# One gather per layer into slots sorted by expert, range copies for each pair, and expert outputs accumulated in four PSUM banks

## The reference, cut to what matters

```python
for l in range(DEPTH):                      # 2 layers
    h = h + mixer_l(rms_norm(h, ln_mix[l]))
    xn = rms_norm(h, ln_ffn[l])
    h = h + hier_moe(xn, ...)
# hier_moe: top-1 of 4 groups, top-2 of its 8 experts, 32 experts in all
g_sel = argmax(xt @ w_rg + b_rg)
top_w, top_i = top_k(softmax(e_logits of g_sel), 2)
for e in range(32):
    hh = silu(xt @ w_gate[e]) * (xt @ w_up[e])      # 1024 -> 512
    y = y + combine[:, e:e+1] * (hh @ w_down[e])    # 512 -> 1024
```

## Time and profile before

| | us |
|---|---|
| median of 3 runs (1334.38 to 1337.42) | 1336.81 |
| the profiled execution's own time | 1337.13 |
| its span, first to last instruction | 1335.3 |
| gather of layer 0 starts, last scatter of layer 0 ends | 169.08, 673.93 |
| gather of layer 1 starts, last scatter of layer 1 ends | 832.56, 1328.28 |
| TensorE busy | 1275.1 (95%) |
| VectorE, ScalarE, GpSimd busy | 287.7, 189.7, 162.6 |
| moved by DMA | 444.44 MB |

### The profile page before, as it was taken

The page is one execution under the profiler, slowest core; times in us unless marked ns, Lnnn a source line. Parts: engine busy times, 40 slices in busy tenths (PEclk is TensorE's granted clock), DMA queues, the critical chain, the costliest instruction groups (busy, mean ns, idle before and its releaser), DMA issues.

```text
span 1335.3 us, 15013 instructions
## 1 busy us (share of the span) xinstructions
PE 1275.1 (95%) x5526; PEld 630.2 (47%) x5526; DVE 287.7 (22%) x621; ACT 189.7 (14%) x445; POOL 162.6 (12%) x392
## 2 busy tenths in 40 slices
PE   6999899999999999999989998999999999999997
PEld 4776464343434344334367764643434343443432
DVE  1664411111111111111122335011111111111112
ACT  1244111010101011201012231110101010110101
POOL 3002011101010102010010000111010101121000
PEclk9999989999999999999999999999999999999999
DMA  6944578899999999799793335659999999999980
GB/s 226 386 180 166 213 321 319 355 413 414 409 423 406 422 409 423 308 415 401 305 358 126 127 142 214 278 234 403 408 423 411 422 403 423 414 423 409 408 342 32
DMA packets 65684, 444.44 MB, mean 333 GB/s; under 512 B 7188, under 2 KB 10384, under 8 KB 13024
## 3 DMA queue, kind: packets, MB, share of 16 engines
q1 hardware_dynamic: 63728, 438.09, 81.1%
q0 software_dynamic: 1040, 2.61, 0.7%
q10 hardware_dynamic: 864, 3.02, 0.6%
HBM read 442.59 MB, written 1.09 MB: 332 GB/s over the span
## 4 chain that ended last, share of the span: by engine, by line
PE 94%; DVE 3%; ACT 1%; issue 1%; DMA 1%; POOL 0%; DVEq 0%; POOLq 0%; SPq 0%; ACTq 0%
PE PS L1342 34%; PE PS L1351 17%; PE PS L1362 9%; PE PS L1094 9%; PE PS L1321 8%; PE PS L1210 4%; PE PS L1098 3%; PE PS L1308 2%; PE PS L1378 1%; PE PS L1106 1%; PE PS L1165 1%; PE PS L1073 1%; DVE mix L1020 1%; PE PS L1194 1%; ACT gain_att L712 1%
## 5 line engine op out<-in xcount | busy, mean ns | idle before, releaser
L1342 PE MATMUL PS<-ring,xT 128*64 128x512 f32 x1392 | 312.8, 595 | 0.0
L1342 PEld LDWEIGHTS PS<-ring,xT 128*64 128x64 f32 x1392 | 96.1, 137 | 206.9 <-issue 206.9
L1351 PE MATMUL PS<-ring,gain_att 128*64 128x512 f32 x768 | 171.4, 595 | 7.5 <-ACT gain_att L712 7.5
L1362 PE MATMUL PS<-mix 128*128 128x512 f32 x256 | 126.8, 618 | 1.7 <-ACT mix L721 1.7
L1094 PE MATMUL PS<-xT,ring 128*128 128x256 f32 (+1 forms) x512 | 120.8, 389 | 0.7 <-issue 0.7
L1034 DVE TENSOR_TENSOR h<-PS,h 128x512 f32<-128x512 f32 x128 | 88.5, 692 | 143.0 <-PE PS L1362 142.8
L1321 PE MATMUL PS<-mix,xn 128*128 128x256 f32 x448 | 116.2, 412 | 0.0
L1321 PEld LDWEIGHTS PS<-mix,xn 128*128 128x128 f32 x448 | 109.4, 335 | 11.4 <-issue 11.4
L1094 PEld LDWEIGHTS PS<-xT,ring 128*128 128x128 f32 (+1 forms) x512 | 96.1, 192 | 22.1 <-issue 7.2
L1351 PEld LDWEIGHTS PS<-ring,gain_att 128*64 128x64 f32 x768 | 53.0, 137 | 108.8 <-issue 97.3
L460 POOL TENSOR_TENSOR sm<-sm 128x1 f32<-128x1 f32 x46 | 8.9, 193 | 743.8 <-PE PS L1384 730.5
(11 more groups left out here) (194 smaller groups left out, 886.7 us busy)
## 6 DMA issues: line engine op xcount, KB each, us to landing
ring<-in_moe_w_up SPq DMA_DIRECT2D x96, 1024.0 KB, 9.6
ring<-in_moe_w_down SPq DMA_DIRECT2D x96, 1024.0 KB, 10.3
ring<-in_moe_w_gate SPq DMA_DIRECT2D x94, 1024.0 KB, 8.6
wo<-in_moe_w_gate SPq DMA_DIRECT2D x34, 1024.0 KB, 9.6
wo<-in_moe_w_down SPq DMA_DIRECT2D x30, 1024.0 KB, 12.0
wo<-in_moe_w_up SPq DMA_DIRECT2D x24, 1024.0 KB, 8.2
ring<-in_c_w_in SPq DMA_DIRECT2D x12, 1024.0 KB, 8.5
ring<-in_ab_w_in SPq DMA_DIRECT2D x9, 1024.0 KB, 10.1
```

Source lines behind the costliest of these rows:

```text
L1342: last = mm(PS[e * SLOTS:(e + 1) * SLOTS, 2 + part, :], (xg if n < 2 else xg2)[:, k, x_cols], w[e][:, kk, :], start=(k == 0), stop=(k == N ...
L1351: last = mm(PS[e * SLOTS:(e + 1) * SLOTS, 6 + b, :], hidT[:, k, e * SLOTS:(e + 1) * SLOTS], w[e][:, 512 * b:512 * b + 512], start=(k == 0) ...
L1362: mm(PS[:, b], pickT[:, t], ye[:, 512 * b:512 * b + 512], start=True, stop=True).then_inc(s_sca[l], 1)
```

## The change

Names: PICKED = 512 is the number of picks of a layer. `acts` is one tile that holds `xn`, `xT` and `kon` behind one another. `xg_all` lies over `xn` and `xT` and has 8 blocks of 512 slots.

- VectorE counts the picks of each expert, sums them up to the start of each expert's range, and from this gets for each token the two slots of its two picks (`pos`, `late`, `early`). It writes `pick_all`, 512 columns for each of the two token tiles.
- TensorE gathers all picks of the layer once, 8 blocks with 2 matmuls of 512 columns each. ScalarE and VectorE copy the blocks in turn to `xg_all`.
- For each pair ScalarE copies, for each of the two experts, 64 columns of all 8 blocks from the start of its range to `xg` (`window`). The start is read into a register of ScalarE. Columns behind the range belong to the next experts; `pickw` has zeros there.
- The wide fills, `pick2`, `xg2` and the gathers of pair 1 are gone; GpSimd makes only `pickw`.
- The scatters accumulate in banks 0, 1, 4 and 5 over all pairs of the layer. Those of pair i run in pair i + 1, two ahead of the turns of `hid` and two behind. The four adds to `h` come once, at the end of the layer. The turns now go to banks 2 and 3.
- No up chunk of the next pair is drawn forward. `xT` is no single-use place any more, so four are left.
- The turned bias of layer 1 comes one pair later (LAST 3 instead of 4).
- Rows of the weights are laid out so that block k of `xn` is 128 neighbouring columns instead of every eighth column. This is done on the host for the large weights; the router weights `wr` are now read in pieces of 16 and 128 bytes instead of 128 bytes and 1 KB.

The core of the diff, a line of "..." where something is left out:

```diff
-LAST = 4
-AHEAD = 2
+LAST = 3
+PICKED = SEQ * TOP_EXPERTS
...
+GATHER_BANK = (0, 1, 2, 3, 6, 7, 0, 1)
+BLOCK = (4, 5, 6, 7, 0, 2, 1, 3)
+Y_BANK = (0, 1, 4, 5)
...
+        xg_all = acts[:, 0:NK * PICKED].rearrange("p (b n) -> p b n", b=NK)
...
-                sp.wait_ge(s_lg[l], 2)
-                chunk(l, 1, 1, OUT_CHUNKS + ONCE - 2)
...
-                pool.dma_start(wr[:, :, 0:GROUPS], w_rg[l].rearrange("(p k) g -> p k g", k=NK)).then_inc(s_wr[l], 16)
-                pool.dma_start(wr[:, :, GROUPS:ROUTES], w_re[l].rearrange("(p k) g -> p k g", k=NK)).then_inc(s_wr[l], 16)
+                pool.dma_start(wr[:, :, 0:GROUPS], w_rg[l].rearrange("(k p) g -> p k g", k=NK)).then_inc(s_wr[l], 16)
+                pool.dma_start(wr[:, :, GROUPS:ROUTES], w_re[l].rearrange("(k p) g -> p k g", k=NK)).then_inc(s_wr[l], 16)
...
+                def window(base, e, blocks=slice(0, NK)):
+                    src = acts[:, bass.ds(base, NK * PICKED)].rearrange("p (b n) -> p b n", b=NK)
+                    act.activation(xg[:, blocks, e * SLOTS:(e + 1) * SLOTS], src[:, blocks, 0:SLOTS], ACT.Copy).then_inc(s_xg[l], 1)
+                def experts(i, first=False, final=False):
+                    if not final:
+                        base = [base_of(i + 1, e) for e in range(AT_ONCE)]
                     act.wait_ge(s_used[l], i * CHUNKS + UP_CHUNKS)
                     if not first:
                         act.wait_ge(s_ht[l], i)
                     act.activation(hid, PS[:, 2], ACT.Silu).then_inc(s_si[l], 1)
-                    if first:
-                        gathered_copy(1, 0)
-                    if odd and not final:
-                        wide_copy(i + 1, 0)
-                        wide_copy(i + 1, 1)
+                    if not final:
+                        act.wait_ge(s_used[l], i * CHUNKS + 2 * UP_CHUNKS)
+                        for e in range(AT_ONCE):
+                            window(base[e], e)
                     act.wait_ge(s_ht[l], i + 1)
-                    act.activation(hidT, PS[:, 4].rearrange("p (k n) -> p k n", k=NF), ACT.Copy).then_inc(s_hT[l], 1)
-                    if first:
-                        gathered_copy(1, 1)
-                    if odd and not final:
-                        wide_copy(i + 1, 2)
-                        wide_copy(i + 1, 3)
+                    act.activation(hidT, PS[:, 2].rearrange("p (k n) -> p k n", k=NF), ACT.Copy).then_inc(s_hT[l], 1)
                     act.wait_ge(s_used[l], i * CHUNKS + CHUNKS)
...
+                link(dve.tensor_copy(counts, PS[:, 5, 0:EXPERTS]))
+                link(dve.tensor_tensor_scan(starts, counts, counts, 0.0, ALU.add, ALU.max))
+                link(dve.tensor_tensor(starts, starts, counts, ALU.subtract))
+                link(dve.tensor_tensor(pos, chose, starts.unsqueeze(1).broadcast_to((P, NT, EXPERTS)), ALU.mult))
+                link(dve.tensor_tensor(pos, pos, rank, ALU.add))
+                link(dve.tensor_reduce(late, pos, AX.X, ALU.max))
+                link(dve.tensor_reduce(both, pos, AX.X, ALU.add))
+                link(dve.tensor_tensor(early, both, late, ALU.subtract))
+                link(dve.tensor_scalar(early2, early, -float(SEQ), None, ALU.add))
+                iota = kon[:, 4 * P:4 * P + SEQ]
                 for t in range(NT):
...
+                    a, b = pick_all[:, t, 0:SEQ], pick_all[:, t, SEQ:2 * SEQ]
+                    dve.tensor_scalar(a, iota, late[:, t:t + 1], None, ALU.is_equal)
+                    link(dve.tensor_scalar(b, iota, float(SEQ), late[:, t:t + 1], ALU.add, ALU.is_equal))
+                    dve.scalar_tensor_tensor(a, iota, early[:, t:t + 1], a, ALU.is_equal, ALU.add).then_inc(s_pk, 1)
+                    dve.scalar_tensor_tensor(b, iota, early2[:, t:t + 1], b, ALU.is_equal, ALU.add).then_inc(s_pk, 1)
+                for j in range(MAX_PASSES):
+                    ins = dve.tensor_scalar(bases_f[0:1, j * EXPERTS:(j + 1) * EXPERTS], starts[0:1], float(SLOTS * j), float(PICKED),
+                                            ALU.add, ALU.min)
+                link(ins)
+                dve.tensor_copy(bases, bases_f[0:1]).then_inc(s_base, 1)
+                weights(l, 1, s_wt)
...
+                def gather(k):
+                    if k >= 6:
+                        pe.wait_ge((s_xa, s_xd)[k % 2], 4 * l + 1)
+                    for t in range(NT):
+                        if k == 0:
+                            pe.wait_ge(s_pk, 4 * l + 2 * t + 2)
+                        last = mm(PS[:, GATHER_BANK[k]], xn[:, t, k * P:(k + 1) * P], pick_all[:, t], start=(t == 0), stop=(t == NT - 1))
+                    last.then_inc(s_g, 1)
...
+                def scatter(q, first=False, final=False):
                     t, b = q // 2, q % 2
...
+                    last = mm(PS[:, Y_BANK[q]], pickT[:, t], ye[:, 512 * b:512 * b + 512], start=first, stop=final)
+                    if final:
+                        last.then_inc(s_sca[l], 1)
+                def ye_there(i):
+                    pe.wait_ge(s_ya[l], i + 1)
+                    pe.wait_ge(s_yd[l], i + 1)
+                    pe.wait_ge(s_pkT[l], i + 1)
+                def pair(i, n, rounds=0, first=False, second=False):
+                    for c in range(2 * UP_CHUNKS):
                         up_chunk(i, first, n, rounds, c)
...
+                    if not first:
+                        ye_there(i - 1)
+                        scatter(0, second)
+                        scatter(1, second)
                     pe.wait_ge(s_hi[l], i + 1)
+                    for k in range(NF):
+                        last = nc.tensor.transpose(PS[:, 2, k * P:(k + 1) * P], hid[:, k * P:(k + 1) * P], ident)
+                    last.then_inc(s_ht[l], 1)
                     if not first:
...
+                        scatter(2, second)
+                        scatter(3, second)
                     pe.wait_ge(s_pw[l], i * PICKS + PICKS)
...
                     for t in range(NT):
...
+                        last = nc.tensor.transpose(PS[:, 3, t * P:(t + 1) * P], pickw[:, t], ident)
                     last.then_inc(s_pkt[l], 1)
...
                     pe.wait_ge(s_hT[l], i + 1)
...
                     for k in range(NF):
                         down_chunk(n, rounds, k)
...
+                for k in range(NK):
+                    gather(k)
                 pair(0, 0, first=True)
...
+                pair(1, 1, second=True)
```

More of the change, by code:

```diff
@@ L70 @@
 PICKS = NT * AT_ONCE
-WIDE = 2 * AT_ONCE
-FILLS = 4
 UNITS = 16
@@ L258, in build @@
         now, now_w, now_slots = at(4936, NT, AT_ONCE), at(4940, NT, AT_ONCE), at(4944, SLOTS)
-        xg2 = xT
-        pick2 = at(1536, NT, WIDE * SLOTS)
-        now2, now2_w = at(5008, NT, WIDE), at(5016, NT, WIDE)
+        pos, counts, starts = at(3584, NT, EXPERTS), at(3648, EXPERTS), at(3680, EXPERTS)
+        bases_f, bases = at(3712, MAX_PASSES * EXPERTS), drop0[0:1, :].bitcast(INT32)
+        late, both, early, early2 = (at(5008 + 2 * j, NT) for j in range(4))
         isc, cand, over, same = (bias[:, 12 + j] for j in range(4))
@@ L500, in pick_rows @@
                     pool.tensor_copy(now_slots, kon[:, bass.ds(i // PAIRS * SLOTS + 4 * P, SLOTS)]).then_inc(s_now[l], 1)
[L501 to L508 removed]
+                    pool.wait_ge(s_now[l], i * 3 + 3)
+                    if not first:
+                        pool.wait_ge(s_pkt[l], i)
                     carry_waits(1)
@@ L1015, in _, with experts @@
                 ranks(l)
-                def experts(i, first):
+                for k in range(1, NK, 2):
+                    gathered_copy(l, k)
+                def experts(i):
                     dve.wait_ge(s_used[l], i * CHUNKS + 2 * UP_CHUNKS)
@@ L1353, in down_chunk @@
                     last.then_inc(s_used[l], 1)
-                def scatter(i, q):
+                def scatter(q, first=False, final=False):
                     t, b = q // 2, q % 2
-                    if q < 2:
-                        pe.wait_ge((s_ya, s_yd)[b][l], i + 1)
-                    else:
-                        pe.wait_ge(s_add[l], i * 4 + (q - 1))
-                    mm(PS[:, b], pickT[:, t], ye[:, 512 * b:512 * b + 512], start=True, stop=True).then_inc(s_sca[l], 1)
-                def pair(i, n, rounds=0, first=False, final=False):
-                    for c in range(0 if first else AHEAD, 2 * UP_CHUNKS):
-                        up_chunk(i, first, n, rounds, c)
-                    if first:
-                        gather(1, 0)
-                    if n % 2 == 1 and not final:
-                        wide_fill(i + 1, 0)
-                        wide_fill(i + 1, 1)
+                    last = mm(PS[:, Y_BANK[q]], pickT[:, t], ye[:, 512 * b:512 * b + 512], start=first, stop=final)
+                    if final:
+                        last.then_inc(s_sca[l], 1)
@@ L1380, in pair @@
                     pe.wait_ge(s_pw[l], i * PICKS + PICKS)
-                    if not first:
```

(20 more changed lines are left out.)

237 lines of the change are left out of this document (86 added, 151 removed).

## The result

| | before | after |
|---|---|---|
| median, us | 1335.6 (1334.19 to 1337.42, 4 runs) | 1271.35 (1270.6 to 1273.3, 4 runs) |
| the profiled execution's time and span | 1337.13, 1335.3 | 1270.6, 1268.4 |
| TensorE busy | 1275.1 (95%) | 1166.0 (92%) |

The ratio is **0.952, 95% interval 0.9502 to 0.9539**: faster, as forecast, and inside the range of 1246 to 1285. The predicted 1259 is 12 us too low. In spans it is 1257.2 against 1268.4, 11.2 us.

What follows compares the result with a forecast made beforehand. It took TensorE and the loads as full together, the loads binding after the change: span 1335.3 - 35.9 (layer 1) - 42.2 (layer 0) = 1257.2, time 1258.7, stated as 1259 us, range 1246 to 1285.

Steps and rivals of the forecast that it cites:

- The loads become the bound: Expert stages: loads at 29.8 us a pair bind once TensorE's 30.5 us pair gets cheaper.
- TensorE stays the bound: Rival, 10%: expert pairs cost TensorE 28.5 us through windows read at a register-held column; time 1295.
- the falling clock: Rival, 4%: in each layer's last six or seven pairs TensorE waits for chunks and drops to half clock; 1401.
- slower windows: Within the 10% rival of a TensorE bound: a ScalarE window copy would take 3.4 us, not 0.6.
- half clock throughout the gather: Rival, 10%: the gather at each stage's start costs 10.8 us a layer more; time 1281.
- TensorE's pair, 25.8: TensorE's work for one pair in the expert stage after the change: 25.8 us, against 30.5 before.
- Start of a stage: Before the first up chunk: gather starts 3.3 us later, includes 3.0 for half clock; first up chunk 12.2 later.
- First use: Start of layer 0's first up chunk, which moves from 176.99 to 189.2 us.
- The hole: Load stream: the 17th load waits for the place of pair 1's first down chunk; 2.1 us lost in layer 1.
- The stream and its tail: 172 chunks take 427.4 us a layer, then 6.4 us from last landing to the end of the last scatter.
- The seam: Between layer 0's last scatter and the next mixer's projection: 6.3 us as before, no wait for loads.
- The load rate: Load stream: 422 GB/s, 2.485 us a chunk; the skill's 358 GB/s would give 2.93 and a sum near 1412.

Runs made afterwards that it cites:

- halved loads: Changed kernel loading only half the columns of each down chunk from pair 1 on; 1191.6 us in one run.
- the windows twice: Changed kernel with each window copied twice by ScalarE from pair 2 on, first into an unused part of mix; 1272.46 us, ratio 0.9515.
- the warm kernel: Changed kernel with seven dummy matmuls a layer where TensorE waits for VectorE between the choice and the gather; 1266.4 us, ratio 0.9482.
- the kernel with early scatters: Changed kernel with the seven dummy matmuls and, in each layer's last pair, the previous pair's scatters behind up chunks 1 and 3; 1263.89 us, ratio 0.9451.

## Why the prediction was right, and where its size was off

**The loads become the bound.** Right: no scatters cost 7 us less, not 109; halved loads went down to TensorE's floor of 1191.6. The rival that TensorE stays the bound is out, and so are the falling clock, slower windows (the windows twice changed nothing) and half clock throughout the gather (it was back at 1.00 from 804).

**TensorE's pair, 25.8.** 25.04. The step priced the turns by their busy time, 0.69 + 0.35, where the chain has 0.44 + 0.22; two scatters by 1.91 each time, where the second two take 1.72; and the up chunks by the stage's first pair, 13.88, where a later one takes 13.73. It changed nothing in the result, as the loads bind, but it moved two of my expectations by some 23 us.

**Start of a stage.** +3.3 in front of the gather: in layer 1 it was 11.07 us from the route's matmuls (788.39) to the gather (799.46), before 7.8, so +3.3. Layer 0's route ran at half clock (0.50 from 159 to 162 us; 3.54 in place of 1.95) and got +5.1. The gather's 16.8 were 16.25: half clock over the first 4.5 us, as in the gather of before, where 6 had been put in, while the matmuls at full clock came out dearer than 13.8 (14.5 in the warm kernel).

**The first part of the stream.** First use 187.63 against 189.2. The mixer of layer 0 ended 2.8 us earlier (158.73 against 161.50 for the route's matmuls), the start cost 1.8 more than forecast, the gather 0.5 less. The 2.8 stand in no term of the sum and are luck for the prediction. Whether the change gives them or the execution does is not shown: in the eleven profiles of the changed kernel and its variants these matmuls start between 156.7 and 161.8, seven times near 159, and in the kernel before and its variant at 161.5 and 161.8. The hole was 1.9 against 2.1.

**The stream and its tail: the term that was off**, by +7.5 us in layer 0 and +5.8 in layer 1. From the first up chunk to the end of the last scatter it took 450.0 (187.63 to 637.65) and 445.5 us (815.70 to 1261.21) where 442.5 and 439.7 stood in the sum. The parts in layer 1:

- The load of the next gain vector, 0.5 MB on ScalarE's queue, stands inside the stage and was not in the 172 chunks: 1.2 us. This size is worked out from its bytes, not tried alone.
- The rate was 421.4 GB/s over the stage, not 422: 172 chunks take 428.0, not 427.4: 0.6.
- The stream ends slowly: about 3 (see the rows of 1247 to 1251 above). Together 4.8, and the kernel without scatters shows 4.7. (Counted in that kernel: it moved 181.06 MB in the stage, 0.70 more than the chunks, 1.7 us; and its slow end with the start of TensorE behind it costs 2.5.)
- The order behind the last up chunk. By the kernel without scatters and the hole, the wait for the last down chunk would end 435.9 + 1.9 after the first up chunk, at about 1253.5, while TensorE comes to that chunk only at 1249.66 + 5.3 = 1255.0, for it does four scatters first: 1.4. The trace bears this out, the loads are nearly over from 1252 on, and none runs from 1253:

```profile
1252.00:1253.00 1.00, 1.00 (x6) 0.29 (x4) 0.00 (x0) 0.00 (x0) 0.00 (x0) 1.00 0.04 16
```

With the scatters early, 1.6 and 0.6 came back; in that kernel's layer 1 the hole was 0.6 larger than here (355 and 384 GB/s from 850 to 870).

In all 6.2, less 0.2 for the smaller hole, against 5.8 measured. In layer 0 the kernel with early scatters has the end of the wait 442.0 us after the first up chunk, 5.8 over the forecast. The gain vector and the rate are 1.8 of them, as above. The 2 MB of raw bias are 1.0: around them the rate was 359 GB/s for seven microseconds. And from 188 to 630, when that wait ended, the core moved some 184.1 MB, 1.1 MB more than the 172 chunks, the bias and the gain vector, so about 2.7 us went to loads that stand behind the last down chunk in the queue. That is 5.5; the order behind it is the other 1.6.

What was off is the step that put the last landing at "854.5 + 2 + 2.1 + 427.4" and hung only its own down chunk behind it: it took the end of a stream of loads as bytes over rate, and TensorE as waiting for it.

**The seam.** From the last scatter to the projection it was 6.3 us (637.65 to 643.94), as forecast. From the last scatter of layer 0 to the first up chunk of layer 1 it took 178.1 us, where 178.8 stood in the sum: -0.7, most of it the gather.

The sum closes: -1.6 (first use) + 7.5 (layer 0) - 0.7 (seam) + 5.8 (layer 1) + 0.2 (end) = 11.2 us, the difference of the spans. Without the earlier end of layer 0's mixer the prediction would have been some 14 us too low, still inside its range.

**The load rate.** The trace holds 420 to 423 GB/s for some 360 us a layer, with this one core at work. The figure of about 358 in the Trainium skill, "DMA: Bandwidth & Descriptors", section "Where 436 GB/s comes from", lies well below that; the measurement decides, and the sum by that figure (1412) is refuted.

## What to carry to other kernels

When two resources are full together, relieve one and the time falls to the other and no further: here another 109 us of TensorE's work removed gave 7. Once the loads bind, what counts is their two ends: everything in front of the first freed buffer counts one to one, and behind the last landing the consumer's own order does. Between them, look for the buffer that only the consumer frees early on: part of what is saved in bytes turns into a hole in the stream there (4.8 of 10.0 us in layer 1).

## What the runs showed that I had not expected

- A stream of 1 MB loads over 16 DMA engines ends over some 3 to 4 us though it ran at 1.01 up to there: shares 0.67, 0.41, 0.12, 0.04 in the kernel with early scatters, 0.60, 0.42, 0.12 in the one without scatters.
- An idle TensorE can be filled for profit: seven dummy matmuls a layer in its waits kept the granted clock at 1.00 through layer 1's ranks and gather, and the gather at 14.5 us in place of 16.2.
- The changed kernel's executions differ by up to 7 us (1268.31 to 1275.36), while the stage's length repeats to 0.1 us in two profiles. In the profiles the first gather starts between 167.8 and 174.5 us: much of the spread lies in the mixers, and small edits are better read from lengths in the trace than from the totals.
